# High and low parts in the gate products of a recurrence, one unit later in the block

## The chip, the cores and the metric

The kernel runs on one core of one Trainium2 chip. The metric is the device time of one execution in microseconds (us), as the median of several runs. The engines are TensorE (PE; its weight loads are listed as PEld), VectorE (DVE), ScalarE (ACT), GpSimd (POOL) and SyncE (SP), whose queue issues most DMAs. Each works through its own queue in order and waits for others on semaphores.

## What is computed

One residual layer of a streaming encoder, for 256 tokens of 2048 channels, in float32:

```python
proj = rmsnorm(x) @ w_in      # FoX q, k, v, forget logits | LRU x, LRU gate | memory q | merge gates
xr = causal_depthwise_conv(lx, w_lru_conv, b_lru_conv)                # width 4
# rg_lru, per block of 128 channels (8 blocks):
r      = sigmoid(xb @ w_a + b_a)
i_gate = sigmoid(xb @ w_x + b_x)
log_a  = 8 * r * log_sigmoid(lam)
u      = sqrt(-expm1(2 * log_a)) * (i_gate * x)
h[t]   = exp(log_a)[t] * h[t-1] + u[t]
y_lru  = h * gelu(lg)
# y_fox: forgetting attention, 8 heads; y_mem: cross-attention to 256 memory tokens, 4 heads
merged = sum(sigmoid(gate_logits) * (branches @ w_branch))
x = x + merged @ w_out
x = x + (gelu(u_act) * u_val) @ w_ffn_down       # ConvGeGLU, hidden 5632
```

The change touches the two products `xb @ w_a` and `xb @ w_x` and what stands around them.

## The kernel before

**Units.** All large weights are streamed in 568 units of 512 KB. SP loads unit u into one of four `raw` slots once DVE has finished unit u-4 (`load`, and the loop at L358 to L362). ACT copies `raw` to a float32r tile as the high part (`split`, L676), once PE has finished unit u-4; DVE subtracts it from `raw` to give the low part (`split`, L1035) and raises `lo_done`. PE waits for `lo_done` and then runs the unit (`group` for the narrow phases, `wide_unit` for the wide ones). A narrow unit (lru, gate, branch, up) is 16 matmuls, half of 512 columns and half of 256; a wide unit (mem, q, k, v, out, down) is 12 matmuls of 512 columns. Main results collect in `psG`. A narrow group of units is taken out by ACT's copy of the lower half (`copy_low`, L684) and DVE's addition (`add_low`, L1046).

**Order.** The phases are listed in `PHASES`: the memory's v and k, q of the memory attention, four lru blocks (8 units each, two groups of 4: the x branch to `lx_pad`, the gate branch to `lru["lg"]`), v, k and q of the FoX attention, then gates and branches by quarters, out, up, down.

**Side steps.** Everything else is a side step, hung behind the split of a unit on ACT and DVE by the tables `steps_at`, and behind a unit's matmuls on PE by `hooks`. For the lru instance m (block m of 256 channels) the offsets count from the first unit of block m+1, and units of the next block have the offsets 0 to 7. In `iteration("lru", "lru", i)` the block's index k runs from 4 to 11; the steps with offset k of instance i-1 come first and then those with offset k-8 of instance i. Behind split k = 8 stands, for example, step 0 of instance i.

The steps of instance m before the change:

| offset | ACT | DVE |
|---|---|---|
| 0 | `conv0_`: the newest tap of the convolution | |
| 1 | | `taps`: the three others, six instructions |
| 3 | `gelu_square` | |
| 5 | `gate_tanh`: from the gate products in `psM` | |
| 6 | | `log_a` (also `ix`) |
| 7 | `exps`, `gelu_tanh` | |
| 8 | | `decay_sq` |
| 9 | `lru_root` | `recurrence`, `gated_y` |
| 10 | `lru_hi`: high part of Y | `lru_lo`: low part of Y |

PE's part is `gates_` behind unit 1 of the next block: four float32 matmuls of 128x128 weights and 256 columns (L524). The profile records each as two, and gives all matmuls the line of their helper, L373. `gates_` waits for the gate weights in `lru["rg"]` (`rg_in`) and for `lru_taps`.

**POOL** has one queue for all four instances (`lru_instance`): `load_gates` (wait for the gates of the instance before, then two DMAs of 128 KB, L1530), `gelu_poly`, `gelu_cube`, and `a_sq` (waits for `exps`). The load for instance m stands right behind `a_sq` of instance m-1.

**The last instance** runs into the v groups. `decay_hooks` puts the logits of the forget gates on PE behind unit 1 of the second v group. They wait until DVE and ACT have counted every step of the four instances, `lru_hi` and `lru_lo` of the last among them. In that stretch `run_units` does first the copy out of `psG` that falls on a unit (L1040, behind the last unit of a v group by four), then the split and then the side steps.

Of the kernel before, what the change touches and what calls it, by code (L numbers as in the profile page):

```python
# [6 lines left out]
ALU = mybir.AluOpType  # L7
ACT = mybir.ActivationFunctionType
F32 = mybir.dt.float32
F32R = mybir.dt.float32r  # L10
AX_X = mybir.AxisListType.X

P = 128
T = 256
# [102 lines left out]
def side_count(kind, m, engine, step):  # L117

    return m * LEN[kind][engine] + (BASE[kind][engine] + (STEP[kind][engine][step] if step else 0))


def at(const, i, coef):

    return const if i is None else i * coef + const


def hybrid_layer_kernel(nc, xT, x_rows, memT, first_data, par, shapes_const, w_units, w_ff, w_rg, out):
    with ExitStack() as ctx:
# [4 lines left out]
        def sb(name, shape, offset, dt=F32):  # L133
            return nc.alloc_sbuf_tensor_at(name, shape, dt, offset=SB0 + int(offset))

        def sem(name):
            return ctx.enter_context(nc.semaphore(name))
# [18 lines left out]
        def wide_before(g):  # L156

            return sum(name in WIDE for name, _, _, _ in GROUPS[:g])
# [5 lines left out]
        M0, G_0, T0 = 145 * KB + 256, 177 * KB + 256, 193 * KB + 256  # L164
# [38 lines left out]
        lru = {}  # L203
        for n in ["lg", "rg", "xr", "ra", "a", "aa", "tn", "ix", "hs", "gg"]:
            shape = [P, 2, 2, P] if n == "rg" else [P, 2, T]
            lru[n] = sb(f"lru_{n}", shape, _o)
            _o += 2 * KB

        dec = {n: sb(f"dec_{n}", [8, T], G_0 + (12 + j) * KB) for j, n in enumerate(["z", "e", "u", "r"])}
        dec_l = sb("dec_l", [8, T], T0 + 2 * KB + 512)  # L210
# [48 lines left out]
        psM = ctx.enter_context(nc.psum_tensor("psM", [P, 4, 512], F32))  # L259
# [10 lines left out]
        gain_in, par_in, const_in, ff_in, rg_in = sem("gain_in"), sem("par_in"), sem("const_in"), sem("ff_in"), sem("rg_in")  # L270
# [11 lines left out]
        lam_act, lam_dve = sem("lam_act"), sem("lam_dve")  # L282
        c_out, c_in = sem("c_out"), sem("c_in")
        lru_conv0, lru_taps = sem("lru_conv0"), sem("lru_taps")
        gate_ready = sem("gate_ready")
        gated, acc_added, merged_hi, merged_lo = sem("gated"), sem("acc_added"), sem("merged_hi"), sem("merged_lo")
        x_tok_in = sem("x_tok_in")
# [14 lines left out]
        def columns(w):  # L302

            return slice(w * 512, (w + 1) * 512)
# [5 lines left out]
        def is_zero(m):  # L310

            return isinstance(m, int) and m == 0

        def f32(ap):
            return ap.bitcast(F32)
# [55 lines left out]
        def _(pe):  # L371
            def mm(*a, **kw):
                return nc.tensor.matmul(*a, skip_group_check=True, **kw)  # L373
# [62 lines left out]
            def side_waits(**need):  # L436
                for e, v in need.items():
                    if not is_zero(v):
                        pe.wait_ge(side[e], v)

            def done(ins):
                ins.then_inc(side["pe"], 1)
# [72 lines left out]

            def lru_hooks(m):
                def gates_():
                    pe.wait_ge(rg_in, at(32, m, 32))
                    pe.wait_ge(lru_taps, at(3, m, 3))

                    side_waits(act=side_count("lru", m - 1, "act", "gate_tanh"))
                    for j in range(2):
                        for b in range(2):
                            ins = mm(psM[:, j, b * T:(b + 1) * T], lru["rg"][:, j, b], lru["xr"][:, b], start=True, stop=True)  # L524
                    done(ins)
                return {1: gates_}

            def decay_hooks():
                def logits():
# [44 lines left out]
            with pe.Fori(1, 4) as i:  # L574
                plain("lru", i, lru_hooks(i - 1))
            wide_group("v", 0, x_op, lru_hooks(3))
            wide_group("v", 1, x_op, decay_hooks())
            wide_group("kq", 0, x_op, {})
# [61 lines left out]
            for t in range(2):  # L640
                for k in range(2):
                    x_hl = hidden_op(FT - 2 + k)
                    for x_part, w_part in ((0, 0), (0, 1), (1, 0)):
                        ins = mm(psG[:, 2 + t, :], x_hl[:, x_part, t * P:t * P + P], W_low[:, s, 2 * k:2 * k + 2, w_part],
                                 start=False, stop=k == 1 and x_part == 1)
# [23 lines left out]
        def _(act):  # L669
# [16 lines left out]
            def wait(**need):  # L686
                for e, v in need.items():
                    if not is_zero(v):
                        act.wait_ge(side[e], v)

            def done(ins):
                ins.then_inc(side["act"], 1)
# [79 lines left out]
            L = lru  # L772

            def conv0_(kind, m):
# [5 lines left out]
                                               bias=p1("b_lconv", m * 2 + b), scale=p1("w_lconv", m * 2 + (3 * BT + b)))  # L780
                ins.then_inc(lru_conv0, 1)

            def gelu_square(kind, m):
                wait(**{e: side_count("lru", m, e, None) for e in ("pe", "dve", "act", "pool")})
                act.wait_ge(evac_done, at(G0["lru"] + 2, m, 2))
                done(nc.scalar.activation(L["gg"][:], L["lg"][:], ACT.Square))

# [29 lines left out]
            def decay_ln(kind, m):  # L817
# [2 lines left out]

            softmax = {7: [exp], 10: [weights_copied], 11: [attention_hi]}
            steps_at = {"normed": {3: [norm_squares]}, "turned": {0: [turned_copied]}, "mem": softmax, "fox": softmax,
                        "lru": {0: [conv0_], 3: [gelu_square], 5: [gate_tanh], 7: [exps, gelu_tanh], 9: [lru_root], 10: [lru_hi]},
                        "decay": {6: [decay_exp], 8: [decay_ln]}}
            hooks = build_hooks(steps_at)

# [201 lines left out]
        def _(dve):  # L1028
            V = nc.vector
# [18 lines left out]
            def wait(**need):  # L1048
                for e, v in need.items():
                    if not is_zero(v):  # L1050
                        dve.wait_ge(side[e], v)

            def done(ins):
                ins.then_inc(side["dve"], 1)
# [58 lines left out]
            L = lru  # L1113

            def taps(kind, m):
                for n in (2, 1, 0):
# [6 lines left out]
                                                     L["xr"][:, b], ALU.mult, ALU.add)  # L1123
                    ins.then_inc(lru_taps, 1)

            def log_a(kind, m):
                wait(act=side_count("lru", m, "act", "gate_tanh"))
                for b in range(2):
                    ins = V.tensor_scalar(L["ra"][:, b], L["ra"][:, b], 1.0, ls4[:, bass.ds(m * 2 + b, 1)], ALU.add, ALU.mult)
                done(ins)  # L1130

                done(V.scalar_tensor_tensor(L["ix"][:], L["ix"][:], 1.0, L["xr"][:], ALU.add, ALU.mult))
# [72 lines left out]
            def decay_bias1(kind, m):  # L1205
# [2 lines left out]

            steps_at = {"normed": {3: [norm]}, "mem": {7: [row_max, weights], 11: [attention_lo]},
                        "fox": {7: [row_max, weights], 11: [attention_lo]},  # L1210
                        "lru": {1: [taps], 6: [log_a], 8: [decay_sq], 9: [recurrence, gated_y], 10: [lru_lo]},
                        "decay": {5: [decay_z], 7: [decay_one_plus], 8: [decay_inverse], 9: [decay_c], 14: [decay_bias0], 15: [decay_bias1]}}
            hooks = build_hooks(steps_at)

# [224 lines left out]
            for w in range(2):  # L1439
                ins = V.memset(up_pad[w][:, :, 0:2], 0.0)  # L1440
# [54 lines left out]
            for w in range(4):  # L1495
                per = FT // 2
                for u in range(U0["down"] + per * w + 4, U0["down"] + per * (w + 1) + 4):
                    if u == U0["down"] + per * (w + 1) + 3 and w < 3:
                        dve.wait_ge(pe_units, u - 3)
                        b = 2 * (w % 2)  # L1500
# [10 lines left out]
        @block.gpsimd  # L1511
        def _(pool):
            G = nc.gpsimd

            def wait(**need):
                for e, v in need.items():
                    if not is_zero(v):
                        pool.wait_ge(side[e], v)

            def done(ins):  # L1520
                ins.then_inc(side["pool"], 1)


            def load_gates(m):

                if is_zero(m):
                    pool.wait_ge(pe_units, U0["mq"])
                wait(pe=side_count("lru", m, "pe", None))
                for j in range(2):
                    G.dma_start(lru["rg"][:, j], w_rg[j, bass.ds(m * 2, 2)].rearrange("b n c -> n b c")).then_inc(rg_in, 16)  # L1530

            L = lru
            def lru_instance(m):
                load_gates(m)
                wait(act=side_count("lru", m, "act", "gelu_square"))
                done(G.tensor_scalar(L["gg"][:], L["gg"][:], GELU_C, 1.0, ALU.mult, ALU.add))
                wait(pool=side_count("lru", m, "pool", "gelu_poly"))
                done(G.tensor_tensor(L["gg"][:], L["gg"][:], L["lg"][:], ALU.mult))
                wait(act=side_count("lru", m, "act", "exps"))
                done(G.tensor_tensor(L["aa"][:], L["a"][:], L["a"][:], ALU.mult))  # L1540


            for m in range(4):
                lru_instance(m)

            wait(dve=side_count("decay", 0, "dve", "c"))
            G.dma_start(c_rows, dec["u"][:]).then_inc(c_out, 16)
            pool.wait_ge(c_out, 16)
            G.dma_start(c_all[:], c_rows.rearrange("(a h) t -> a h t", a=1).to_broadcast([P, 8, T])).then_inc(c_in, 16)

            pool.wait_ge(x_scaled, 4)
            G.dma_start(x_tok[:], x_rows).then_inc(x_tok_in, 16)

            for w in range(3):
                pool.wait_ge(evac_done, G0["down"] + w + 1)
                G.dma_start(out_rows[:, :, columns(w)], x_tok[:, :, columns(w)]).then_inc(out_stored, 16)
            pool.wait_ge(out_stored, 48)
# [96 lines left out]
```

## Time and profile before

| | |
|---|---|
| median of 3 runs | 1622.5 us (1622.48 to 1623.05) |
| the profiled execution | 1623.35 us |
| its span, first to last instruction | 1621.6 us |
| instructions | 24765 |
| ACT busy, DVE busy | 869.1 us, 1052.3 us |
| granted TensorE clock | full (1.000) over the whole span |

A timeline row gives the start and the length of an operation or of a row of like ones (count x); consecutive operations overlap a little, so what an operation takes of its queue is the distance between starts. The list of waits says whom an engine waited for. The chain of waits goes back from the last instruction, and its pieces have no overlap, so their lengths are what PE spent. For a DMA issue the last number is the median time in us from issue to landing.

### The profile page before, as it was taken

The page shows a single profiled execution, that of the slowest core. Times are in us where ns is not written, and L with a number is a line of the kernel's source. Part 1 is how long each engine was busy: PE and PEld are TensorE (multiplying, and loading weights), DVE is VectorE, ACT ScalarE, POOL GpSimd, SP SyncE. Part 2 cuts the span into 40 slices and gives each one's busy share as a digit, 9 for nine tenths or more (in the row PEclk, how much of TensorE's full clock was granted, in tenths as well). Part 3 has the DMA queues.
Part 4 walks back from the last instruction along what each step waited for, and adds up shares of the span by engine and source line. Part 5 has one row for each costly group of instructions (what it writes and reads, how often), then busy time and mean ns, then how long its engine had stood idle before and what let it go on. Part 6 is the DMA issues. An engine that isn't in the chain of part 4 may idle for free.

```text
span 1621.6 us, 24765 instructions
## 1 busy us (share of the span) xinstructions
PE 1616.1 (100%) x8564; PEld 1390.7 (86%) x8564; DVE 1052.3 (65%) x1257; ACT 869.1 (54%) x1192; POOL 25.6 (2%) x30
## 2 busy tenths in 40 slices
PE   9999999999999999999999999999999999999999
PEld 7888888888888888888888888888888888888887
DVE  6865688655656575564755777777777777544443
ACT  6665676466545554555554655555555555433332
POOL 0000121000000000000000000000000000000000
PEclk9999999999999999999999999999999999999999
DMA  8554455655455556555565555655555655565663
GB/s 341 193 194 146 160 171 192 243 191 163 162 184 196 190 181 198 190 190 192 186 196 183 181 182 182 207 190 183 197 181 182 207 191 186 203 203 193 205 207 115
DMA packets 85281, 309.59 MB, mean 191 GB/s; under 512 B 9832, under 2 KB 10352, under 8 KB 84976
## 3 DMA queue, kind: packets, MB, share of 16 engines
q1 hardware_dynamic: 83952, 303.14, 55.7%
q0 software_dynamic: 1136, 5.78, 1.0%
q8 instruction: 32, 0.52, 0.1%
q14 instruction: 17, 0.14, 0.0%
q10 hardware_dynamic: 144, 0.01, 0.0%
HBM read 306.78 MB, written 2.11 MB: 190 GB/s over the span
## 4 chain that ended last, share of the span: by engine, by line
PE 97%; DMA 1%; DVE 1%; SPq 0%; ACT 0%; issue 0%
PE psG L373 94%; PE psM L373 2%; DMA raw<-w_units 1%; DVE W L1035 1%; PE psM L458 0%; PE psM L611 0%; ACT W L676 0%; PE psM L494 0%; PE psM L492 0%; SPq L355 0%; SPq L334 0%; DVE sq_mem L1263 0%; DVE mem_v L1040 0%; DVE sq_mem L1261 0%; DVE sq_x L1258 0%
## 5 line engine op out<-in xcount | busy, mean ns | idle before, releaser
L1035 DVE TENSOR_TENSOR W<-raw,W 128x1024 fp32r<-128x1024 f32 x566 | 688.0, 1228 | 375.4 <-ACT W L676 373.0
L373 PE MATMUL psG<-X,W 128*128 128x512 f32 (+1 forms) x4864 | 845.3, 336 | 0.0
L373 PEld LDWEIGHTS psG<-X,W 128*128 128x128 f32 x4864 | 740.9, 188 | 101.1
L676 ACT ACTIVATE W<-raw 128x1024 fp32r<-128x1024 f32 x566 | 589.8, 1054 | 390.3 <-PE psG L373 373.7
L373 PE MATMUL psG<-W,hidden 128*128 128x512 f32 x1056 | 239.5, 389 | 0.0
L373 PEld LDWEIGHTS psG<-W,hidden 128*128 128x128 f32 x1056 | 198.1, 188 | 41.1
L373 PE MATMUL psG<-W,X 128*128 128x512 f32 x768 | 178.7, 392 | 0.0
L373 PEld LDWEIGHTS psG<-W,X 128*128 128x128 f32 x768 | 143.4, 188 | 29.5
L684 ACT ACTIVATE low<-psG 128x512 f32<-128x512 f32 x100 | 59.7, 597 | 147.5 <-PE psG L373 147.5
L373 PE MATMUL psG<-Y,W 128*128 x768 | 133.1, 335 | 0.0
L373 PEld LDWEIGHTS psG<-Y,W 128*128 128x128 f32 x768 | 116.9, 188 | 15.9
L1455 DVE SCALAR_TENSOR_TENSOR up_c<-up_pad,par_sb,up_c 128x256 f32<-128x256 f32 x176 | 77.5, 482 | 42.3 <-ACT up_c L988 36.3
L373 PE MATMUL psG<-W,XM 128*128 128x512 f32 x384 | 88.7, 391 | 0.8 <-ACT XM L843 0.6
L373 PE MATMUL psG<-W,merged 128*128 128x512 f32 x384 | 88.0, 390 | 0.0
L373 PEld LDWEIGHTS psG<-W,XM 128*128 128x128 f32 x384 | 71.6, 188 | 16.6 <-ACT XM L843 0.9
L373 PEld LDWEIGHTS psG<-W,merged 128*128 128x128 f32 x384 | 71.8, 188 | 14.7
L988 ACT ACTIVATE up_c<-up_pad,par_sb 128x256 f32<-128x256 f32 x88 | 48.2, 595 | 60.8 <-DVE up_pad L1447 60.8
L1014 ACT ACTIVATE hidden<-up_c 128x512 f32 (+1 forms) x22 | 13.9, 632 | 65.3 <-DVE up_c L1484 65.3
L1046 DVE TENSOR_TENSOR up_pad<-psG,low 128x512 f32<-128x512 f32 x44 | 30.4, 692 | 24.8 <-ACT low L684 24.6
L1046 DVE TENSOR_TENSOR gates<-psG,low 128x512 f32<-128x512 f32 x24 | 16.6, 692 | 27.2 <-ACT low L684 27.2
L1046 DVE TENSOR_TENSOR yd<-psG,low 128x512 f32<-128x512 f32 x24 | 16.6, 692 | 22.5 <-ACT low L684 22.5
L1447 DVE TENSOR_TENSOR up_pad<-up_pad,rstd 128x512 f32<-128x512 f32 x44 | 30.3, 688 | 0.8
(191 smaller groups left out, 553.5 us busy)
## 6 DMA issues: line engine op xcount, KB each, us to landing
raw<-w_units SPq DMA_DIRECT2D x566, 512.0 KB, 3.3
xs<-xT SPq DMA_DIRECT2D x4, 512.0 KB, 9.4
x_tok<-x_rows POOLq DMA_DIRECT2D x1, 2048.0 KB, 12.9
mem_raw<-first_data SPq DMA_DIRECT2D x3, 512.0 KB, 5.1
mem_raw<-memT SPq DMA_DIRECT2D x3, 512.0 KB, 7.7
out<-x_tok POOLq DMA_DIRECT2D x3, 512.0 KB, 3.8
lru_rg<-w_rg POOLq DMA_DIRECT2D x8, 128.0 KB, 4.1
c_all<-c_rows POOLq DMA_DIRECT2D x1, 1024.0 KB, 7.2
```

The costliest lines, as they stand in the source:

```text
L373: return nc.tensor.matmul(*a, skip_group_check=True, **kw)
L676: nc.scalar.activation(slots_of(u)[:, s, :, 0], raw[:, s], ACT.Copy).then_inc(hi_done, 1)
L684: nc.scalar.activation(low[:, g % 2], psG[:, b:b + 2, T:], ACT.Copy).then_inc(low_copied, 1)
L988: ins = nc.scalar.activation(up_c[w][:, t], up_pad[w][:, t, 2:], ACT.Identity, bias=p1("b_fconv", i * 2 + (w * FT + t)), scale=p1("w_fconv ...
L1014: nc.scalar.activation(hidden[:, bass.ds(i * 2, 2), 0, :], up_c[1][:], ACT.Copy).then_inc(hidden_hi, 1)
L1035: V.tensor_tensor(slots_of(u)[:, s, :, 1], raw[:, s], f32(slots_of(u)[:, s, :, 0]), ALU.subtract).then_inc(lo_done, 1)
L1046: V.tensor_tensor(dst, psG[:, b:b + 2, 0:T], low[:, g % 2], ALU.add).then_inc(evac_done, 1)
L1447: V.tensor_tensor(up_pad[w][:, :, 2:], up_pad[w][:, :, 2:], rstd2.rearrange("p (a t) -> p a t", a=1).to_broadcast([P, 2, T]), ALU.mult).th ...
L1455: ins = V.scalar_tensor_tensor(up_c[w][:, t], up_pad[w][:, t, n:n + T], p1("w_fconv", i * 2 + (n * 2 * FT + w * FT + t)), up_c[w][:, t], A ...
```

## The change

Before, the gate products are float32 matmuls, straight from `lru["rg"]` and `lru["xr"]`. After, weights and input are first taken apart in a high part (rounded to float32r, on ACT) and a low part (the rest, on DVE), and each product is the sum of three float32r matmuls: high by high, high weights by low input, low weights by high input. For this there are two new tiles, four semaphores and four new steps at offsets 1 and 2. `gates_` moves from unit 1 to unit 2 of the next block, and all steps from `gate_tanh` on move one offset later; `gelu_square` stays and waits for `y` of the instance before in place of its last step. POOL's load of the gate weights waits for the low part of the instance before in place of its gates. The convolution's steps stay.

```diff
+        lru_w = sb("lru_w", [P, 2, 2, 2, P], M0 + 89 * 256, F32R)
+        lru_x = sb("lru_x", [P, 2, 2, T], M0 + 105 * 256 + 64, F32R)
...
@@ -515,15 +518,17 @@
-                    pe.wait_ge(rg_in, at(32, m, 32))
-                    pe.wait_ge(lru_taps, at(3, m, 3))
+                    pe.wait_ge(lru_w_lo, at(1, m, 1))
+                    pe.wait_ge(lru_x_lo, at(1, m, 1))
 
                     side_waits(act=side_count("lru", m - 1, "act", "gate_tanh"))
                     for j in range(2):
                         for b in range(2):
-                            ins = mm(psM[:, j, b * T:(b + 1) * T], lru["rg"][:, j, b], lru["xr"][:, b], start=True, stop=True)
+                            for w_part, x_part in ((0, 0), (0, 1), (1, 0)):
+                                ins = mm(psM[:, j, b * T:(b + 1) * T], lru_w[:, j, b, w_part], lru_x[:, b, x_part],
+                                         start=w_part + x_part == 0, stop=w_part == 1)
                     done(ins)
-                return {1: gates_}
+                return {2: gates_}
@@ -780,8 +785,18 @@
+            def gate_weights_hi(kind, m):
+                act.wait_ge(rg_in, at(32, m, 32))
+                for j in range(2):
+                    ins = nc.scalar.activation(lru_w[:, j, :, 0], L["rg"][:, j], ACT.Copy)
+                ins.then_inc(lru_w_hi, 1)
+
+            def gate_input_hi(kind, m):
+                act.wait_ge(lru_taps, at(3, m, 3))
+                nc.scalar.activation(lru_x[:, :, 0], L["xr"][:], ACT.Copy).then_inc(lru_x_hi, 1)
+
             def gelu_square(kind, m):
-                wait(**{e: side_count("lru", m, e, None) for e in ("pe", "dve", "act", "pool")})
+                wait(**{e: side_count("lru", m, e, None) for e in ("pe", "act", "pool")}, dve=side_count("lru", m - 1, "dve", "y"))
...
-                        "lru": {0: [conv0_], 3: [gelu_square], 5: [gate_tanh], 7: [exps, gelu_tanh], 9: [lru_root], 10: [lru_hi]},
+                        "lru": {0: [conv0_], 1: [gate_weights_hi], 2: [gate_input_hi], 3: [gelu_square], 6: [gate_tanh], 8: [exps, gelu_tanh], 10: [lru_root], 11: [lru_hi]},
@@ -1123,6 +1138,16 @@
+            def gate_weights_lo(kind, m):
+                dve.wait_ge(lru_w_hi, at(1, m, 1))
+                for j in range(2):
+                    ins = V.tensor_tensor(lru_w[:, j, :, 1], L["rg"][:, j], f32(lru_w[:, j, :, 0]), ALU.subtract)
+                ins.then_inc(lru_w_lo, 1)
+
+            def gate_input_lo(kind, m):
+                dve.wait_ge(lru_x_hi, at(1, m, 1))
+                V.tensor_tensor(lru_x[:, :, 1], L["xr"][:], f32(lru_x[:, :, 0]), ALU.subtract).then_inc(lru_x_lo, 1)
...
-                        "lru": {1: [taps], 6: [log_a], 8: [decay_sq], 9: [recurrence, gated_y], 10: [lru_lo]},
+                        "lru": {1: [taps], 2: [gate_weights_lo, gate_input_lo], 7: [log_a], 9: [decay_sq], 10: [recurrence, gated_y], 11: [lru_lo]},
@@ -1525,7 +1550,8 @@
                 if is_zero(m):
                     pool.wait_ge(pe_units, U0["mq"])
-                wait(pe=side_count("lru", m, "pe", None))
+                else:
+                    pool.wait_ge(lru_w_lo, m)
```

## Rows read from the trace of the kernel before

**Rows 1.** Page, part 1: busy us, share of the span, instructions.

```profile
PE 1616.1 (100%) x8564; PEld 1390.7 (86%) x8564; DVE 1052.3 (65%) x1257; ACT 869.1 (54%) x1192; POOL 25.6 (2%) x30
```

**Rows 2.** What PE waited for, whole run: us in total, times, longest.

```profile
PE psM L373 <- DVE ones L1222: 1.1, 1, 1.1
PE psG L373 <- ACT XM L843: 0.6, 1, 0.6
PE psG L373 <- DVE mem_v L1040: 0.3, 1, 0.3
```

**Rows 3.** Chain of waits, in order of time: start us, us, what, records.

```profile
107.53 16.35 PE psG L373 x72
...
209.04 1.73 PE psM L373 x8
210.77 22.09 PE psG L373 x128
```

**Rows 4.** Timeline of ACT: start us, us, operation, count, idle before.

```profile
210.35 1.28 ACT L676 ACT_TABLE_LOAD   x1
...
213.56 0.82 ACT L792 ACTIVATE lru_ra<-psM,half_ba 128x256 f32<-128x256 f32 x2
214.27 0.83 ACT L792 ACTIVATE lru_ix<-psM,half_bx 128x256 f32<-128x256 f32 x2
...
218.93 0.62 ACT L803 ACTIVATE lru_gg<-lru_gg 128x512 f32<-128x512 f32 x1
219.45 1.05 ACT L676 ACTIVATE W<-raw 128x1024 fp32r<-128x1024 f32 x1
220.40 1.08 ACT L779 ACTIVATE lru_xr<-lx_pad,par_sb 128x256 f32<-128x256 f32 x2
...
222.93 1.28 ACT L807 ACT_TABLE_LOAD   x1
224.23 0.72 ACT L807 ACTIVATE lru_aa<-lru_aa,eps 128x512 f32<-128x512 f32 x1
```

**Rows 5.** Timeline of DVE, same columns.

```profile
224.98 0.69 DVE L1141 TENSOR_TENSOR lru_ix<-lru_ix,lru_aa 128x512 f32<-128x512 f32 x1 [0.81 <-ACT lru_aa L807]
...
228.21 2.93 DVE L1122 SCALAR_TENSOR_TENSOR lru_xr<-lx_pad,par_sb,lru_xr 128x256 f32<-128x256 f32 x6
231.05 1.22 DVE L1035 TENSOR_TENSOR W<-raw,W 128x1024 fp32r<-128x1024 f32 x1
232.18 0.68 DVE L1157 TENSOR_TENSOR Y<-lru_hs,Y 128x512 f32 x1
232.78 0.69 DVE L1046 TENSOR_TENSOR lru_lg<-psG,low 128x512 f32<-128x512 f32 x1
```

**Rows 6.** Timeline of POOL, same columns.

```profile
195.28 1.04 POOL L1540 TENSOR_TENSOR lru_aa<-lru_a 128x512 f32<-128x512 f32 x1 [10.46 <-ACT lru_tn L799]
196.26 1.50 POOL L1530 DMA_DIRECT2D lru_rg<-w_rg  x2
...
219.10 1.97 POOL L1540 TENSOR_TENSOR lru_aa<-lru_a 128x512 f32<-128x512 f32 x1 [6.44 <-ACT lru_tn L799]
```

**Rows 7.** DMA issues from 181, 197, 222 us, 209 to 233; gate-load extremes.

```profile
lru_rg<-w_rg POOLq DMA_DIRECT2D x2, 128.0 KB, 2.9
...
lru_rg<-w_rg POOLq DMA_DIRECT2D x2, 128.0 KB, 4.4
...
lru_rg<-w_rg POOLq DMA_DIRECT2D x2, 128.0 KB, 4.5
...
raw<-w_units SPq DMA_DIRECT2D x8, 512.0 KB, 4.3
...
DMA to landing us min/median/max: 2.7/4.1/5.4
```

**Rows 8.** Timelines of ACT and DVE ahead of the decay logits.

```profile
269.36 1.06 ACT L676 ACTIVATE W<-raw 128x1024 fp32r<-128x1024 f32 x1 [1.28 <-PE psG L373]
...
276.86 0.68 DVE L1157 TENSOR_TENSOR Y<-lru_hs,Y 128x512 fp32r<-128x512 f32 x1
```

More of the change, by code:

```diff
@@ L284, in hybrid_layer_kernel @@
         lru_conv0, lru_taps = sem("lru_conv0"), sem("lru_taps")
+        lru_w_hi, lru_w_lo, lru_x_hi, lru_x_lo = sem("lru_w_hi"), sem("lru_w_lo"), sem("lru_x_hi"), sem("lru_x_lo")
         gate_ready = sem("gate_ready")
```

## Prediction

> **What bounds the kernel now.** I read the page's busy shares first. TensorE (PE) is busy for 1616.1 of 1621.6 us, VectorE (DVE) for 65% and ScalarE (ACT) for 54% [rows 1]. The list of PE's waits has only three, 2.0 us in all, at the start of the kernel [rows 2]. So the span is PE's own work, and this change can act in two ways only: by what it takes off or adds to PE's queue, or by making PE wait where it doesn't now. The chain of waits gives PE's prices: eight gate records in 1.73 us, then eight units (128 records) in 22.09 us, so 2.76 us for a narrow unit; a wide stretch of 72 records of 512 columns takes 16.35 us, 0.227 us each [rows 3]. In a narrow unit eight 512-column matmuls cost 8 x 0.227 = 1.82 us, which leaves 0.94 us for the eight of 256 columns: 0.118 us each. Next I read ACT, DVE and GpSimd (POOL) over one block, 203 to 233 us, since PE's slack is kept by them. There the tightest supply is the split of unit 2 of the next block: DVE starts it at 231.05 and ends it at 232.27 [rows 5]; PE's run of eight units from 210.77 ends at 232.86 and the gates take 1.73 us more [rows 3], so PE needs it at 234.6. The slack is 2.3 us, in a kernel whose waits are otherwise nil.
>
> **PE's own work.** Removed: four gate steps of eight records, 4 x 1.73 = 6.92 us. Added: 4 x 12 matmuls of 256 columns. No row has twelve of them in a row; the pairs inside a narrow unit go at 0.118 us, and every one there has a weight load of its own. 12 x 0.118 = 1.41 us a step. The bounds are half of a 512-column one, 0.1135 us, and 0.216 us, the rate of the old gate records of the same width: 1.36 to 2.6 us. I take 1.41, as it is the same form. Gain: 4 x 0.32 = 1.3 us. That is all that the change can give; nothing else on PE shrinks.
>
> **Added work on ACT and DVE, by price.** ACT gets per instance two copies of 256 elements and one of 512. Operations of 512 cost 0.52 us from start to start (218.93 to 219.45), of 1024 0.95 (219.45 to 220.40) [rows 4], so 256 about 0.32: 0.65 + 0.54 us. DVE gets two subtractions of 256 and one of 512: 1024 takes 1.13 us from start to start, 512 0.60 (231.05, 232.18, 232.78) [rows 5], so 256 about 0.33: 0.67 + 0.60 us. Both have the room on average. What matters is where they stand.
>
> **The moved steps and the load of the weights.** I number steps by the unit whose split they follow: 7 is unit 7 of block i, 8 to 11 are units 0 to 3 of the next, as the code does. t is 0 when PE ends unit 3 of block i. ACT's split k can't start before PE ends unit k-4, so split 7 falls at 0, 8 at 2.8, 9 at 5.5, 10 at 8.3. The exponentials of instance m-1 go from step 7 to step 8. POOL's queue is in order: the square of a, then the two DMAs with the gate weights of instance m. The load's new wait is met early, but it still stands behind the square, which waits for the exponentials. Before, nobody but PE needed these weights, at the gates some 12 us later. Now ACT waits for them at step 9, one unit after the exponentials, with split 10 and all behind it in the queue. In order, for the first instance affected (m=1):
> - ACT: lower half of psG copied 0.05 to 0.55, split 7 to 1.5; DVE adds, splits 7 and has log a ready at 3.4.
> - ACT: split 8 from 2.8, exponentials 3.8 to 4.9, gelu tanh and first tap to 6.3, split 9 to 7.3.
> - POOL: the square 5.0 to 6.0 (1.04 us at 195.28, when DVE stood idle part of the time, 1.97 us at 219.10 beside a DVE split, [rows 6]). In the new order DVE has ended split 8 at about 5.1, so I take 1.04.
> - The load: from the first issue to both halves landed. The medians of the pairs at 181, 197 and 222 us are 2.9, 4.4 and 4.5 us, and the extremes of all eight issues 2.7 and 5.4 [rows 7]; these lie in the first and the second pair. An issue takes 0.75 us [rows 6]. So the first pair is complete after 0.75 + 2.7 = 3.45 us and the second after 0.75 + 5.4 = 6.1; the third lies between them, at 0.75 + 4.5 = 5.25 or somewhat more. The first had DVE nearly idle beside it. The new place has DVE idle for the first 1.4 us and one or two weight units in flight. I take 5.2 us, by the third pair; the range is 3.45 to 6.1. Landed at 11.2.
> - ACT has waited from 7.3 to 11.25, some 4 us. Then: high weights 0.65, split 10 0.96, table load and gap 1.30, root 0.72 [rows 4]: 14.9.
> - DVE from there: product, scans, gelu product, y: 3.23 us from 224.98 to 228.21 [rows 5]; low weights 0.67, low input 0.68: 19.5, with 0.05 for each hand-over.
> - PE ends unit 10 at 7 x 2.76 = 19.3 and waits for the low input: 0.25 us. Behind it DVE has still to add (0.60) and split 11 (1.23) while the gates take 1.41: 0.34 us more. Then ACT's square waits for that sum, a table load of 1.28 stands at the head of the loop body [rows 4] and split 12 comes 0.3 us late. First instance: 0.9 us.
>
> Second instance (m=2): ACT starts the next block behind. DVE's sum of the other half is there at 20.1; ACT then has the square 0.54, the table load 1.28, three splits of 0.96 and the gate tanh, twice 0.71 = 1.42 [rows 4], with the hand-over 6.2 us, and comes to the psG copy at 26.3. PE, from the gates at 19.6, has ended unit 3 after 1.41 + 0.34 + 2.76 = 4.5 us, at 24.1. ACT is 2.2 us late where it was on time a block before. The exponentials come 1.9 us late by this (split 8 has in part to wait for its raw weights, which SyncE asks for when DVE ends split 4 and which take 4.3 us, [rows 7]), and PE gets 0.3 us of it back in its own wait for split 12. So PE waits 0.25 + 1.6 = 1.9, and 0.34: 2.2 us. Third (m=3): the same, with the table load before the tanh and no wait for split 12: 0.25 + 1.9 + 0.34 = 2.5 us. Instance 0 has its weights early and costs nothing: now its load waits only for the mem projections.
>
> **A later wait, whatever the load does.** The logits of the decay stand behind unit 1 of the second v group and wait for the last low half of y. That moves from step 10 to step 11, behind the copy of v (1.2 us) and a split. Before, from PE's end of unit 37 (split 41 at 269.36 on ACT) to the low half done at 277.54 are 8.2 us [rows 8], with four wide units, 10.9 us, of cover. After: three units, 8.2 us, against 0.05 + 0.96 + 1.30 + 0.72 + 0.05 + 3.23 + 1.14 (v) + 1.14 (split) + 0.68 = 9.3 us. PE waits 1.1 us.
>
> **Sum.** 0.9 + 2.2 + 2.5 + 1.1 = 6.7 us of waits, less 1.3 us: +5.5 us with the rounding. The profiled execution took 1623.35 us (span 1621.6 and 1.75 around it), which gives 1628.9; the median of the runs shown is 0.85 lower, 1622.5, which gives 1628.0. What goes at nothing: the extra copies themselves outside the waits, covered by PE's 2.76 us a unit; without that cover they'd be 1.2 us for ACT and 1.3 us for DVE per instance.
>
> **A rule weighed.** The squares of 1.04 us with DVE idle for a part and 1.97 us beside a split show that POOL and DVE hold each other up, and I price the new square at the lower. The Trainium skill, "SBUF — State Buffer", section "SBUF: two separate sides", says that VectorE with two SBUF inputs and GpSimd lock each other out of one port pair, and that while VectorE runs an instruction of a two-port mode a DMA from GpSimd can't get its descriptors written. The rows of the square agree; whether the landings do is not shown. If they did, it would speak for the earlier landing of the first rival (its sum, not mine), since DVE is idle at the new issue.
>
> **Rivals.**
> - The load comes early. POOL's issues fall into DVE's idle time and the pair lands as at 180.35, complete after 3.45 us. Then all from step 9 on moves 1.75 us forward. The waits of the first two instances are gone, the third leaves 0.4, the logits 1.1: 1.5 - 1.3 = +0.2 us, 1622.7. The point from which it decides: each us of the load is worth 3 us in all, so the sum passes 3.2 us at a completion after 4.4 us. For it: the one undisturbed pair. Against it: two of three pairs at 5.25 and more. Chance 0.27. The Trainium skill, "DMA: Bandwidth & Descriptors", section "Anatomy of one DMA", fits a DMA from GpSimd as 2.0 us plus bytes over 436e3, 2.3 us for 128 KB; by this the pair would be complete at 3.05 us, the third instance's wait would go too, and the estimate is 1622.4. No landing here is below 2.7 us, so the trace does not bear it out beside the weight stream.
> - The long chain. Square at 1.97 and load at 6.1 as in the worst rows: the first instance waits 2.8, the next two 4.1 and 4.4 (split 10 itself becomes late, 1.2 and 1.5), the logits 1.1: 12.3 - 1.3 = +11 us, 1633.5. Chance 0.12.
> - The products don't get cheaper. If twelve separate weight loads go at the old 0.216 us, a step takes 2.6 us, 0.87 more than before; with the waits that gives about +9, 1631.5. Against it: the pairs in a unit. Chance 0.04.
> - A gain. It would need more than 3.2 us off PE; the gates hold 6.9 in all and 5.6 of it come back. Only an effect outside this reading, such as other addresses, could do it. Chance 0.03.
>
> **How the numbers follow.** The forecast, a load complete after 4.4 to 5.8 us, has 0.54 and gives +3.2 to +7.3. 0.2% is 3.2 us, about what a measurement of this kernel can tell from no change. Slower by more than that: 0.54 + 0.12 + 0.04 = 0.70; same: the first rival, 0.27; faster 0.03. The range takes in the first rival's middle and leaves out its lowest part and the long chain's end: 1622.6 to 1633.0.
>
> **What would show it.** Right: ACT idle about 4 us before the high weights, released by the DMA, at three instances and not at the first; PE's waits with the gates released by the low input, then by a split; the logits waiting 1 us for the low half of y; gate steps of 1.4 us. Wrong: landings near 3.5 us, or PE with no waits in 180 to 290 us.

## The result and the profile after

The changed kernel takes 1627.78 us (median of 8 runs, 1626.95 to 1628.59), the kernel before 1622.52 us in the same comparison (8 runs, 1622.41 to 1623.05). The ratio is 1.0031, with a 95% interval of 1.0022 to 1.0040: 5.3 us slower. The profiled execution took 1627.48 us. Its page, header and busy shares:

```profile
span 1625.7 us, 24819 instructions
...
PE 1616.5 (99%) x8580; PEld 1390.5 (86%) x8580; DVE 1057.0 (65%) x1269; ACT 873.9 (54%) x1204; POOL 24.3 (1%) x30
```

PE's busy time hardly moved (1616.1 before, [rows 1]), and the span grew by 4.1 us: PE waits more. PE's list of waits for the whole run answers [rows 2] (us in total, times, longest):

```profile
PE psM L376 <- DVE lru_x L1149: 1.4, 1, 1.4
PE psM L376 <- DVE Y L1182: 1.3, 1, 1.3
PE psM L376 <- DVE ones L1247: 1.1, 1, 1.1
PE psM L376 <- DVE lru_w L1144: 0.9, 1, 0.9
PE psG L376 <- DVE W L1050: 0.7, 3, 0.2
PE psG L376 <- ACT XM L858: 0.3, 1, 0.3
```

The waits for `ones` and `XM` at the start were there before, the one for `mem_v` (0.3 us) is gone; new are waits for the low parts of the gates' input and weights, for three splits and for the low part of y, 4.3 us in all. Where they stand shows PE's timeline (start, length, operation, count, idle before):

```profile
186.97 1.52 PE L376 MATMUL psM<-lru_x,lru_w 128*128 128x256 f32 x12
...
210.41 1.52 PE L376 MATMUL psM<-lru_x,lru_w 128*128 128x256 f32 x12
211.77 3.02 PE L376 MATMUL psG<-X,W 128*128 128x512 f32 x16
...
236.00 1.68 PE L376 MATMUL psM<-lru_x,lru_w 128*128 128x256 f32 x12 [1.36 <-DVE lru_x L1149]
...
240.80 11.33 PE L376 MATMUL psG<-X,W 128*128 128x512 f32 x64 [0.23 <-DVE W L1050]
...
261.17 1.65 PE L376 MATMUL psM<-lru_x,lru_w 128*128 128x256 f32 x12 [0.86 <-DVE lru_w L1144]
...
266.11 16.66 PE L376 MATMUL psG<-W,X 128*128 128x512 f32 x72 [0.22 <-DVE W L1050]
284.06 3.90 PE L376 MATMUL psM<-X,ff_w 128*40 128x512 f32 x16 [1.30 <-DVE Y L1182]
```

The same view of the kernel before:

```profile
185.05 1.89 PE L373 MATMUL psM<-lru_xr,lru_rg 128*128 128x256 f32 x8
...
208.88 1.89 PE L373 MATMUL psM<-lru_xr,lru_rg 128*128 128x256 f32 x8
...
256.48 1.89 PE L373 MATMUL psM<-lru_xr,lru_rg 128*128 128x256 f32 x8
...
279.98 3.86 PE L373 MATMUL psM<-X,ff_w 128*40 128x512 f32 x16
```

The twelve new matmuls of a gate step take 1.36 us (210.41 to 211.77) where the old eight records took 1.73 [rows 3]. From one gate step to the next there were 23.82 us before. After, it is 23.44 for the first (186.97 to 210.41), then 25.59 and 25.17. From the last gates to the logits there were 23.50 us before (256.48 to 279.98); now it is 22.89 us, with one wide unit of 2.73 us less between them, so 25.62 alike. These differences are -0.4, +1.8, +1.4 and +2.1 us, +4.9 in all. With 0.37 us added to each for the cheaper gate step, PE lost 0, 2.1, 1.8 and 2.5 us in the four stretches, 6.4 in all. That is 2.1 more than the list of waits shows: part of a wait hides in rows that are drawn out, as the unit at 211.77, whose follower starts 3.25 us later and not 2.76. The profiled spans differ by less, 4.1, because the execution shown of before reached this stretch 0.8 us later (its first gates start at 185.05, one unit of 2.76 us earlier in the order, the new ones at 186.97). That execution was also 0.85 us above its kernel's median. With that, the profile accounts for 4.9 of the 5.3 us.

What stands behind the waits, on ACT:

```profile
197.57 1.05 ACT L681 ACTIVATE W<-raw 128x1024 fp32r<-128x1024 f32 x1
201.65 0.72 ACT L791 ACTIVATE lru_w<-lru_rg 128x256 fp32r<-128x256 f32 x2 [3.04 <-DMA lru_rg<-w_rg]
202.28 1.05 ACT L681 ACTIVATE W<-raw 128x1024 fp32r<-128x1024 f32 x1
...
227.42 0.73 ACT L791 ACTIVATE lru_w<-lru_rg 128x256 fp32r<-128x256 f32 x2 [3.60 <-DMA lru_rg<-w_rg]
...
252.74 0.73 ACT L791 ACTIVATE lru_w<-lru_rg 128x256 fp32r<-128x256 f32 x2 [3.13 <-DMA lru_rg<-w_rg]
```

and on GpSimd, with the time to landing of all eight DMAs of gate weights below (the 4.3 is one of the first instance's, issued early and waited for by nobody; the six behind the squares took 3.4 to 3.9 us):

```profile
196.23 1.11 POOL L1566 TENSOR_TENSOR lru_aa<-lru_a 128x512 f32<-128x512 f32 x1 [13.52 <-ACT lru_tn L814]
197.29 1.50 POOL L1556 DMA_DIRECT2D lru_rg<-w_rg  x2
...
221.45 1.37 POOL L1566 TENSOR_TENSOR lru_aa<-lru_a 128x512 f32<-128x512 f32 x1 [7.57 <-ACT lru_tn L814]
222.76 1.49 POOL L1556 DMA_DIRECT2D lru_rg<-w_rg  x2
...
248.55 1.49 POOL L1556 DMA_DIRECT2D lru_rg<-w_rg  x2
```

```profile
DMA to landing us min/median/max: 3.4/3.6/4.3
```

ACT ends split 9 at 198.6 and stands still for 3.0 us until the DMA issued at 197.29 has landed, then for 3.6 and 3.1 us in the next two instances. Only behind it come split 10 (202.28), the root, the high part of the input and all that DVE makes of them.

### The profile page after: what moved, and what is told of

Same layout as the page of the kernel before. It is cut to its first block, busy times and chain, and to the rows that moved or that the text cites. A ratio compares the mean times of both kernels' runs of the same rounds, so it can differ in the third digit from the quotient of the medians.

```text
span 1625.7 us, 24819 instructions
## 1 busy us (share of the span) xinstructions
PE 1616.5 (99%) x8580; PEld 1390.5 (86%) x8580; DVE 1057.0 (65%) x1269; ACT 873.9 (54%) x1204; POOL 24.3 (1%) x30
## 4 chain that ended last, share of the span: by engine, by line
PE 96%; DVE 1%; ACT 1%; DMA 0%; issue 0%; POOL 0%; ACTq 0%; DVEq 0%
PE psG L376 94%; PE psM L376 2%; DVE W L1050 0%; PE psM L461 0%; ACT W L681 0%; DMA par_sb<-par 0%; ACT L822 0%; PE psM L616 0%; DMA lru_rg<-w_rg 0%; DVE lru_hs L1169 0%; PE psM L497 0%; ACT lru_aa L822 0%; DVE lru_ix L1166 0%; DVE lru_gg L1175 0%; PE psM L495 0%
```

## The experiments

There are eight, in two sets of four, each set on one chip beside the kernel before: 1622.72 us there in the first (the first four below), 1622.74 us in the second. Differences are against these; the changed kernel's is +5.3 from its own comparison.

### The load issued earlier

```diff
             def lru_instance(m):
-                load_gates(m)
+                if m == 0:
+                    load_gates(m)
...
+                if m < 3:
+                    load_gates(m + 1)
                 wait(act=side_count("lru", m, "act", "exps"))
                 done(G.tensor_tensor(L["aa"][:], L["a"][:], L["a"][:], ALU.mult))
```

> One part of the change undone: GpSimd issues the two gate-weight DMAs of the next instance ahead of the square of a instead of behind it, some 8 us earlier. Theory (ACT waits for these weights at step 9 and so makes splits and low input late): all of PE's waits at gates 2 and 3 and at the splits behind them vanish, the wait of the decay logits (1.1 to 1.3 us) stays; gate steps give 4 x 0.36 = 1.4 us back; the time is that of the kernel before within 0.5 us, 1622.5, or 5.2 us under the changed kernel. Rival (the extra operations on ACT and DVE, or their moved order, make the splits late, whenever the weights land): 1626 or more, with the waits at the gates still there. ACT's wait for the DMA should be nil.

Measured: 1624.69 us (1624.06 to 1625.68), +2.0 instead of the +0.0 expected. PE's waits:

```profile
PE psM L376 <- DVE Y L1182: 1.3, 1, 1.3
...
PE psG L376 <- DVE W L1050: 0.5, 2, 0.2
```

The waits for both low parts are gone, and with them 3.3 us. Counted from the gate step before, the load is issued 9 to 15 us earlier than in the changed kernel, not some 8. ACT no longer waits for the DMA. So the load's place, not the added work, made most of the loss. But 2 us stay, and only 1.3 of them are the logits' wait. The rest lies between the last gates and the logits:

```profile
258.13 1.57 PE L376 MATMUL psM<-lru_x,lru_w 128*128 128x256 f32 x12
...
280.84 3.93 PE L376 MATMUL psM<-X,ff_w 128*40 128x512 f32 x16 [1.30 <-DVE Y L1182]
```

22.71 + 2.73 = 25.44 us against 23.50 before, 1.9 more, or 2.3 with the cheaper gate step: 1.3 at the logits and 1.0 elsewhere, at splits. This second part was not in the theory.

### The high weights taken one step later

```diff
-"lru": {0: [conv0_], 1: [gate_weights_hi], 2: [gate_input_hi], 3: [gelu_square], ...
+"lru": {0: [conv0_], 2: [gate_weights_hi, gate_input_hi], 3: [gelu_square], ...
```

> The load stays late, but ACT takes the high part of the weights one step later (step 10, behind split 10 and the root) instead of step 9. Theory (what costs is that split 10 and the root stand in ACT's queue behind the wait, not that the weights are late): the weights have landed or nearly so when ACT comes to them, low input is ready about 3 us before PE needs it, and the time is 1622.5 within 0.7 us. Rival (lateness of the weights itself sets the end of the low input): still 1625 or more.

Measured: 1623.84 us (1623.49 to 1624.07), +1.1. The load is issued as late as in the changed kernel, but ACT's wait for it, 9.8 us in the changed kernel, is

```profile
ACT lru_w L791 <- DMA lru_rg<-w_rg: 0.4, 1, 0.4
```

So 4.1 of the 5.3 us are gone, though the weights arrive no sooner. What cost was the wait's place in ACT's queue, with split 10 and the root behind it. The rival, that the late weights as such set the end, falls. The theory's 1622.5 was missed by 1.3 us: it left out the logits' wait, which PE's list still shows with 1.3 us.

### The last y one step earlier

```diff
                     for o, steps in offs.items():
+                        if kind == "lru" and m == 3 and o == 11:
+                            o = 10
                         for f in steps:
                             where.setdefault(s + o, []).append((f, kind, m))
```

> Only the last instance's high and low part of y go back from step 11 to step 10, ahead of the copy of v and split 11; all else is as in the changed kernel. Theory: the decay logits no longer wait (1.3 us in the profile of the changed kernel), all other waits stay: 1.3 us under the changed kernel, about 1626.5. Rival (the wait is only PE's share of a lateness that DVE keeps, and comes back at the next split): no change, 1627.8.

Measured: 1626.45 us (1625.21 to 1627.62), +3.7, 1.5 us less than the changed kernel. The logits' wait is nil:

```profile
260.39 1.65 PE L376 MATMUL psM<-lru_x,lru_w 128*128 128x256 f32 x12 [0.71 <-DVE lru_w L1146]
...
281.79 3.88 PE L376 MATMUL psM<-X,ff_w 128*40 128x512 f32 x16
```

From the last gates to the logits it takes 21.40 us, 1.5 less than the 22.89 of the changed kernel. The profiled execution is 1.2 us faster than the median of this run, and some of its other waits are shorter too (0.6 us for the low input where the changed kernel had 1.4), so only this stretch is compared.

### The moved steps alone

This starts from the kernel before and keeps the float32 products; `gelu_square` gets the changed wait too.

```diff
-                return {1: gates_}
+                return {2: gates_}
...
-5: [gate_tanh], 7: [exps, gelu_tanh], 9: [lru_root], 10: [lru_hi]
+6: [gate_tanh], 8: [exps, gelu_tanh], 10: [lru_root], 11: [lru_hi]
...
-6: [log_a], 8: [decay_sq], 9: [recurrence, gated_y], 10: [lru_lo]
+7: [log_a], 9: [decay_sq], 10: [recurrence, gated_y], 11: [lru_lo]
```

> The kernel before with the moved steps alone: gates behind unit 2, all later steps one offset later, but the four float32 products as before, with no high and low parts. Theory: moving costs only the wait of the decay logits, 1.1 to 1.3 us: about 1623.7. Rival A (the moved order itself costs the 5 us): 1626 or more. Rival B (moving is free, and the logits' wait comes from the lateness carried over from the instances before): 1622.5.

Measured: 1624.25 us (1624.07 to 1624.48), +1.5. PE waits once more than before, for y:

```profile
PE psM L373 <- DVE Y L1157: 1.3, 1, 1.3
```

It is the only wait behind the start. So moving the steps costs the logits' wait, 1.3 us in the list and 1.5 in the time, and nothing else that PE would feel. The rest of the loss needs the high and low parts. Rival B falls as well: no lateness was carried over here.

### A second square ahead of the load

```diff
                 wait(act=side_count("lru", m, "act", "exps"))
+                G.tensor_tensor(normed.rearrange("p t c -> p (t c)")[:, 0:512].rearrange("p (b t) -> p b t", b=2), L["a"][:], L["a"][:], ALU.mult)
                 done(G.tensor_tensor(L["aa"][:], L["a"][:], L["a"][:], ALU.mult))
```

> The changed kernel with one suspected cost doubled: a second square of the same size on GpSimd ahead of the one that stands before the load, its result unused. The weights then land 1.1 to 1.4 us later in three instances. Theory (each us of the load's lateness is paid by PE in every one of the three instances): 3.3 to 4.2 us over the changed kernel, 1631.5. Rival (the lateness is absorbed in part, since ACT and DVE catch up between two instances): 1 to 2 us more, 1629.5. The square itself also holds y back, but the root waits for split 10 anyway.

Measured: 1631.14 us (1628.63 to 1632.25, 5 runs), +8.4, 3.1 us more than the changed kernel. GpSimd in the first instance affected, ACT in all three, and PE at the last gates:

```profile
197.41 1.04 POOL L1567 TENSOR_TENSOR lru_aa<-lru_a 128x512 f32<-128x512 f32 x1
198.39 1.50 POOL L1556 DMA_DIRECT2D lru_rg<-w_rg  x2
```

```profile
201.88 0.72 ACT L791 ACTIVATE lru_w<-lru_rg 128x256 fp32r<-128x256 f32 x2 [3.17 <-DMA lru_rg<-w_rg]
...
227.62 0.72 ACT L791 ACTIVATE lru_w<-lru_rg 128x256 fp32r<-128x256 f32 x2 [3.55 <-DMA lru_rg<-w_rg]
...
255.67 0.72 ACT L791 ACTIVATE lru_w<-lru_rg 128x256 fp32r<-128x256 f32 x2 [5.86 <-DMA lru_rg<-w_rg]
```

```profile
264.10 2.19 PE L376 MATMUL psM<-lru_x,lru_w 128*128 128x256 f32 x12 [2.41 <-DVE lru_w L1144]
```

The second square puts the issue off by about 1 us. Three times this would be 3.1 us, which is the measured sum, but the profile doesn't show one us in each instance. In the first two instances the DMAs landed after 2.5 to 3.1 us, where those of the changed kernel took 3.5 to 3.9, so that ACT went on only 0.1 us later, counted from the gate step before (187.07 to 201.88 for 186.97 to 201.65, and 210.51 to 227.62 for 210.41 to 227.42). PE's first two stretches, 23.44 and 25.69 us, are those of the changed kernel within 0.1. In the third instance the pair took up to 5.1 us to land, ACT went on 2.73 us later (236.20 to 255.67 for 236.00 to 252.74), and PE's stretch is 27.90 us for 25.17, also 2.73 longer. The last stretch is 0.7 us longer. So in the one instance in which the weights really came later, PE paid all of it. That each us is paid in each of the three instances is not shown; the sum of 3.1 us is a coincidence as far as this execution goes. The times don't decide between theory and rival either: the interval of the ratio, 1.0036 to 1.0063, spans 4 us.

### The repairs together

The early load with the last y:

> The early load (1624.7 when it was alone) together with the last instance's y one step earlier (which alone gave about 1.3 us). Theory: the two waits have nothing to do with each other and add: 1623.4. Rival (the logits' wait only hides another that ends just behind it): no gain over 1624.7.

Measured: 1623.34 us (1622.76 to 1625.57), +0.6. The late load, the high weights one step later, and the last y:

> The late load with the high weights taken one step later (1623.8 alone) together with the last instance's y one step earlier. Theory: 1.3 us under it, 1622.5, the kernel before within 0.3 us. Rival: no gain, 1623.8.

Measured: 1622.28 us (1621.94 to 1624.26), -0.5. Both edits are those shown above, put together. The last of these can't be told from the kernel before (interval of the ratio 0.9989 to 1.0007). The last y is worth 1.5 us on the changed kernel, 1.4 on the early load and 1.6 on the later high weights: the two effects add.

### A version meant to keep the gain

```diff
             def lru_instance(m):
-                load_gates(m)
+                if m == 0:
+                    load_gates(0)
+                if m < 3:
+                    load_gates(m + 1)
                 wait(act=side_count("lru", m, "act", "gelu_square"))
...
-"lru": {0: [conv0_], 1: [gate_weights_hi], 2: [gate_input_hi],
+"lru": {-1: [gate_weights_hi], 0: [conv0_], 2: [gate_input_hi],
...
-"lru": {1: [taps], 2: [gate_weights_lo, gate_input_lo],
+"lru": {0: [gate_weights_lo], 1: [taps], 2: [gate_input_lo],
...
                 act.wait_ge(rg_in, at(32, m, 32))
+                if not is_zero(m):
+                    wait(pe=side_count("lru", m - 1, "pe", "gates"))
```

with the last y one step earlier as above.

> A version meant to keep the gain: the load of the next instance's gate weights is issued right after the low part of this one's is done, the high and low parts of the weights are made at steps -1 and 0, where ACT and DVE have room, and the last y goes one step earlier. Theory: what is left of PE's waits is some 0.5 us in the last instance, where DVE's splits run beside GpSimd; the gates give back 1.4 us: 1621.8, about 0.9 us under the kernel before. Rival (the added 2.5 us of ACT and DVE work per block can't be hidden in these blocks): 1623 or more.

Measured: 1621.42 us (1620.90 to 1623.39), -1.3, ratio 0.9992 with an interval of 0.9983 to 1.0001. PE's waits are those of the start alone:

```profile
PE psM L376 <- DVE ones L1251: 1.1, 1, 1.1
PE psG L376 <- ACT XM L862: 0.9, 1, 0.9
```

From the last gates to the logits:

```profile
257.36 1.57 PE L376 MATMUL psM<-lru_x,lru_w 128*128 128x256 f32 x12
...
277.82 3.88 PE L376 MATMUL psM<-X,ff_w 128*40 128x512 f32 x16
```

20.46 + 2.73 = 23.19 us against 23.50 before, which is the cheaper gate step and no wait. The median lies under the fastest of 27 runs of the kernel before (1622.42), and the size is near what four gate steps give back, 4 x 0.37 = 1.5 us. The interval of the ratio just reaches 1, so it is faster by the median and by the trace, not beyond doubt by the interval. The 0.5 us that the theory left for the last instance didn't appear. The three edits were made together; what each adds here was not measured apart.

## Why the prediction was right

The forecast was +5.5 us, measured +5.3. The mechanism was the forecast one: a load that ACT comes to wait for, and a late y. That the number came so close is in part luck, since two terms were off by more than a microsecond in opposite directions. By its steps:

- **PE's own work.** 1.41 us for a gate step was forecast, 1.36 measured; the gain is 1.5 us, not 1.3. The price from the pairs of 256 columns held for twelve in a row, each with a weight load of its own.
- **The load on ACT's way.** The chain was right link by link, and its terms were off, in part in ways that cancel. The square took 1.11, 1.37 and 1.37 us, not 1.04. From the first issue until ACT went on it took 4.4, 4.7 and 4.2 us (197.29 to 201.65, 222.76 to 227.42, 248.55 to 252.74), not 5.2. The sum of both, 5.5, 6.0 and 5.6, was taken as 6.2. The landings of 3.4 to 3.9 us lie under those of the busy pairs before [rows 7] and over the 2.7 that the first rival needed. So ACT waited 3.0 to 3.6 us and not 4. The forecast case was a load complete after 4.4 to 5.8 us; 4.4, 4.7 and 4.2 lie at its edge to the first rival. By the prediction's own scale, one us for each us in each instance, the 1.5 us that the three sums fall short would have made it +4.0 us.
- **The waits, instance by instance.** PE lost 0, 2.1, 1.8 and 2.5 us in the four stretches, 6.4 in all. The forecast, cut at the same places, was 0.25, 2.5, 2.5 and 1.4, 6.7 in all (the 0.6 us behind the first gates counted to the second stretch, the 0.3 behind the third to the last). The growth from the first to the second instance, through ACT's late start into the next block, was there: PE ended the unit behind the gates at about 214.8, and ACT came to the psG copy at 216.84, 2 us late where 2.2 was forecast. But the wait for split 12, put at 0.3 us behind the first instance and at nothing behind the third, cost 0.5 us behind each (the starts at 211.77 and 215.02, 237.54 and 240.80, 262.86 and 266.11 lie 3.25 us apart, where a unit takes 2.76 or 2.73).
- **The logits.** 1.1 us forecast, 1.3 measured, and the same 1.3 with the steps moved alone. DVE's queue ahead of it is as was read: copy of v, split, low part of y.

What was mis-sized the other way is the last stretch: 2.5 us for 1.4, 0.5 of it the wait for split 12. The forecast priced DVE's operations there as if GpSimd did not run beside it. DVE's timeline of the changed kernel, behind the last gates and ahead of the logits, and the GpSimd operation beside it:

```profile
262.72 1.10 DVE L1182 TENSOR_TENSOR Y<-lru_hs,Y 128x512 fp32r<-128x512 f32 x1
263.74 4.59 DVE L1050 TENSOR_TENSOR W<-raw,W 128x1024 fp32r<-128x1024 f32 x3
...
281.06 1.22 DVE L1055 COPY v_all<-psG 128x1024 f32<-128x1024 f32 x1
282.20 1.21 DVE L1050 TENSOR_TENSOR W<-raw,W 128x1024 fp32r<-128x1024 f32 x1
283.33 0.68 DVE L1182 TENSOR_TENSOR Y<-lru_hs,Y 128x512 fp32r<-128x512 f32 x1
```

```profile
263.36 1.61 POOL L1564 TENSOR_TENSOR lru_gg<-lru_gg,lru_lg 128x512 f32<-128x512 f32 x1
```

The low part of y at 262.72 takes 1.10 us, while the one at 283.33 takes 0.68, and three splits take 4.59 us, where three at 1.13 from start to start would end after some 3.5. The first of the three alone takes 2.32 us: it starts at 263.74, GpSimd's multiplication ends at 264.97, and the split ends at 266.06, 1.09 us after that, about the time of a whole split. So it looks as if the split did nothing until GpSimd was done. PE, which needed it, went on at 266.11.

The same was there before, with no wait of PE:

```profile
258.86 1.29 POOL L1538 TENSOR_TENSOR lru_gg<-lru_gg,lru_lg 128x512 f32<-128x512 f32 x1
```

```profile
258.89 3.48 DVE L1035 TENSOR_TENSOR W<-raw,W 128x1024 fp32r<-128x1024 f32 x2 [0.59 <-ACT W L676]
```

Again the first split takes 2.34 us and ends 1.08 us after GpSimd. With the steps moved alone, both slow operations of DVE are there (1.10 us for the low part of y, 4.57 for three splits), and PE doesn't wait for them either. What differs is when DVE comes to the three splits, counted from the start of the last gates: 0.1 us before it with the steps moved alone and 0.6 behind it in the last version, both without a wait; 2.4 behind it with the early load and 2.6 in the changed kernel, both with the wait. So the slow split costs PE nothing by itself; it costs where DVE is late, and that needs the added high and low parts in front of it. No run took GpSimd's work away there, so how the 1 us divides between the two is open. That it isn't the load is shown by the early load, where the same 1.0 us stayed.

The first rival, an early landing, was told apart by the landings themselves (3.4 us at the least, so a pair complete after 4.2 to 4.7 us, where the rival had 3.45). The fit of the Trainium skill, "DMA: Bandwidth & Descriptors", section "Anatomy of one DMA", from which the estimate for such a load is 2.3 us, is not borne out beside the weight stream: no landing in the changed kernel is below 3.4 us, and none in the other runs below 2.5. The long chain needed the worst rows of both terms, and the products did get cheaper. The price of that third rival, about +9, is less than its terms as given: 6.7 us of waits and 4 x 0.87 of work are 10.2.

## What to carry to other kernels

When an engine gets a new wait, ask first what is queued behind it and by whom the awaited thing is issued: here a load of two times 128 KB with 12 us of room became a stop of 3 us in front of ScalarE's weight splits, because both its issue and its use moved towards each other. A gain in the bounding engine's own work of 0.1% is lost by one such wait per block. Either issuing the load earlier (3.3 us back) or taking its result one step later in the queue (4.1 us back) undid most of the loss; the gain itself showed most clearly (-1.3 us) when the load was issued a block earlier, the weights' parts were made where both engines had room, and the last y went earlier too. Follow moved steps to the end of the loop too, where the last instance meets other work: one step's delay of the last y cost as much as all cheaper products gave.

## What had not been expected of the hardware

A VectorE operation that meets GpSimd's multiplication seems to wait for its end and then to take its usual time. In five kernels the first split beside it takes 2.30 to 2.34 us where 1.22 is usual, and ends 1.08 or 1.09 us after GpSimd does. The low part of y at 262.72 in the changed kernel ends 0.54 us after a shorter operation of GpSimd (262.52 to 263.28). The other way round, in the kernel before, a multiplication on GpSimd that starts at 235.16, 0.04 us behind a split, takes 2.33 us where 1.30 is usual. So whichever starts first seems to go first. The rows show this only for operations of these kinds.

Weights that came 2.73 us later in one instance of the run with the second square made PE's stretch longer by the same 2.73 us, though in the blocks from 184 to 284 us of the changed kernel VectorE is busy for 79% of the time and ScalarE for 71%: idle time elsewhere in a block doesn't help what stands behind a wait.

The landing of like DMAs of 128 KB varied from 3.4 to 4.3 us in one run of the changed kernel and from 2.5 to 5.1 us in that with the second square. There it made more of a difference than the us by which the issue was put off.
